# Reordered ends of the feed-forward stages and of the gated mixing, one-column bank marks, and named activation tables in a fused two-block layer kernel

## The reference

```python
def conv_ffn(h, w_up, conv_w, conv_b, w_down):            # ffn0
    u = h @ w_up
    up = jnp.pad(u, ((0, 0), (1, 1), (0, 0)))
    u = sum(up[:, j:j + t] * conv_w[j] for j in range(3)) + conv_b
    a, g = jnp.split(u, 2, axis=-1)
    return (jax.nn.gelu(a) * g) @ w_down                   # hidden width 2816
def swiglu_ffn(h, w_in, w_out):                            # ffn1 to ffn4
    gate, up = jnp.split(h @ w_in, 2, axis=-1)
    return (jax.nn.silu(gate) * up) @ w_out
def gmlp_chunk_mix(h, w_uv, v_norm, w_s, b_s, w_o):        # gated mixing
    z = jax.nn.gelu(h @ w_uv)
    u, v = jnp.split(z, 2, axis=-1)                        # 2048 columns each
    v = rms_norm(v, v_norm)
    ws = jnp.where(causal[None], w_s, jnp.zeros_like(w_s))                   # 16 groups of 128 x 128
    sv = jnp.einsum('gts,bcsgd->bctgd', ws, v) + jnp.transpose(b_s)[:, :, None]
    return (u * sv) @ w_o
```

## Time and profile before

| | |
|---|---|
| median of three timed runs | 1980.64 us (1976.95 to 1982.74) |
| the profiled execution | 1974.38 us, of which the span is 1972.2 us |
| mean granted TensorE clock | 0.992 of full speed |
| busy TensorE | 1886.9 us (96% of the span) |
| busy VectorE | 1407.4 us (71%) |
| busy ScalarE | 1044.1 us (53%) |

### The profile page before, as it was taken

One profiled execution on the slowest core, in us unless ns is written; L12 is line 12 of the kernel. 1 busy time (PEld: TensorE's weight loads), 2 busy tenths in 40 slices (PEclk: granted clock), 3 DMA queues, 4 the chain that ended last, 5 costly groups with the idle time before them and its releaser, 6 DMA issues. The chain is left out here.

```text
span 1972.2 us, 40546 instructions
## 1 busy us (share of the span) xinstructions
PE 1886.9 (96%) x16839; PEld 1786.0 (91%) x16844; DVE 1407.4 (71%) x1786; ACT 1044.1 (53%) x1390; POOL 45.7 (2%) x42
## 2 busy tenths in 40 slices
PE   7999998999999999989987999999999998999998
PEld 7998997999998899989886999998999998999997
DVE  6685589767777877798565667778777756557776
ACT  6565576755556444568533554445444555545443
POOL 0000000000000000000052000000000000000000
PEclk9999999999999999999999999999999999999999
DMA  6843333354553455444401434554455453534552
GB/s 219 251 175 127 129 129 113 128 187 172 190 192 139 160 195 188 171 146 149 154 4 46 150 127 173 191 189 174 172 190 192 168 190 117 182 113 174 189 192 107
DMA packets 52316, 313.39 MB, mean 159 GB/s; under 512 B 13536, under 2 KB 13792, under 8 KB 14944
## 3 DMA queue, kind: packets, MB, share of 16 engines
q1 hardware_dynamic: 51760, 308.42, 44.2%
q10 hardware_dynamic: 432, 3.15, 0.4%
HBM read 310.50 MB, written 1.05 MB: 158 GB/s over the span
## 5 line engine op out<-in xcount | busy, mean ns | idle before, releaser
L2138 DVE TENSOR_TENSOR wl<-raw,wh 128x1024 fp32r<-128x1024 f32 x576 | 687.5, 1223 | 375.7 <-ACT wh L1462 372.8
L1462 ACT ACTIVATE wh<-raw 128x1024 fp32r<-128x1024 f32 x575 | 587.8, 1051 | 304.2 <-PE ps L308 154.8
L308 PE MATMUL ps<-pages_r,wh 128*128 128x256 f32 x2480 | 548.1, 287 | 34.1 <-DVE wl L2138 17.7
L308 PE MATMUL ps<-pages_r,wl 128*128 128x256 f32 x1680 | 479.0, 285 | 0.0
L308 PEld LDWEIGHTS ps<-pages_r,wh 128*128 128x128 f32 x2480 | 424.8, 195 | 38.8 <-issue 19.1
L308 PE MATMUL ps<-norm_r,wh 128*128 128x256 f32 x2336 | 430.2, 285 | 2.5 <-DVE norm_r L2202 1.7
L308 PEld LDWEIGHTS ps<-norm_r,wh 128*128 128x128 f32 x2336 | 365.9, 192 | 5.6 <-issue 2.0
L372 PE MATMUL ps<-norm_r,wh 128*128 128x512 f32 x1408 | 355.1, 394 | 2.6 <-DVE wl L2138 1.7
L308 PE MATMUL ps<-norm_r,wl 128*128 128x256 f32 x1184 | 335.0, 283 | 0.0
L308 PEld LDWEIGHTS ps<-pages_r,wl 128*128 128x128 f32 x1680 | 326.1, 194 | 0.0
L372 PEld LDWEIGHTS ps<-norm_r,wh 128*128 128x128 f32 x1408 | 253.5, 189 | 50.4 <-DVE wl L2138 2.4
(11 more groups left out here) (345 smaller groups left out, 1823.8 us busy)
## 6 DMA issues: line engine op xcount, KB each, us to landing
raw<-in_stream SPq DMA_DIRECT2D x287, 1024.0 KB, 4.8
pages<-in_rpb SPq DMA_DIRECT2D x32, 64.0 KB, 6.3
pages<-in_mem SPq DMA_DIRECT2D x2, 512.0 KB, 6.4
raw<-in_stream SPq DMA_DIRECT2D x2, 512.0 KB, 8.4
x<-in_x SPq DMA_DIRECT2D x1, 1024.0 KB, 12.3
pages<-in_mem ACTq DMA_DIRECT2D x1, 1024.0 KB, 5.0
pages<-in_gmlp_b ACTq DMA_DIRECT2D x1, 1024.0 KB, 4.5
pages<-in_gmlp_w ACTq DMA_DIRECT2D x1, 1024.0 KB, 6.6
```

What stands on the lines that cost most here:

```text
L308: mm = pe.matmul(out, left, right, start=start and q == 0, stop=stop and q == 2, skip_group_check=True)
L1462: f(t.wh[(2 * b0 + hf) % PIECE_SLOTS][:], t.raw[b0 % 2][:, hf * 1024:(hf + 1) * 1024], ACT.Copy).then_inc(s["high_done"], 1)
L2138: tt(t.wl[i][:], t.raw[b0 % 2][:, hf * 1024:(hf + 1) * 1024], t.wh[i][:].bitcast(F32), ALU.subtract).then_inc(s["low_done"], 1)
```

## The change

It has four parts. What is computed stays the same, and so do the weight blocks, which come in another order.

1. **Ends of the feed-forward stages.** In the last step of each stage, `early` (the scaling of the gate) goes ahead of the first weight split; the second split is done in halves, and the hidden product goes between them (`between`), ahead of the second half. In ffn0 the step with the taps goes ahead of the first half and the product between the halves. ScalarE's order follows: in ffn0 the gelu and the high copy come right behind the second block's high copies.
2. **Bank marks.** The four matmuls at L469 write one column of each bank.
3. **Gated mixing.** The order of the stream is two gate blocks, eight value blocks, then the other six gate blocks as a new segment `gm_w`. The mixing quarters stand between its blocks, as `MIX_BEHIND` says: two quarters behind the second block, then one, two, two and one behind the following. The mask product stands behind the first two gate evacuations, ahead of the splits of the value blocks. VectorE and ScalarE follow that order: evacuation of a gate block, splits of a later one, then the quarters that are due; VectorE waits for the gelu of gate block q at quarter q, where it waited for all eight before.
4. **Named sets.** `preload_act_table_set("natural_log_exp_and_others")` is put at the start of ScalarE's program, ahead of the Ln of each norm root, of the four logarithms in the `w_in` stage, of the root of the scan's norm, of RWKV's decay exponentials, and in place of the dummy Ln for `rw_o`. It loads one table set that holds both Ln and Exp.

```diff
     ("rw_r", 4, 5), ("lora2", 0, 1), ("mem2_v", 4, 4), ("rw_v", 4, 4), ("rw_o", 4, 4), ("xq0", 4, 4), ("xo0", 4, 4),
-    ("ffn2", 44, 33), ("ffn3", 44, 33), ("gm_u", 8, 8), ("gm_v", 8, 8), ("gm_o", 4, 8),
+    ("ffn2", 44, 33), ("ffn3", 44, 33), ("gm_u", 2, 2), ("gm_v", 8, 8), ("gm_w", 6, 6), ("gm_o", 4, 8),
     ("xq1", 4, 4), ("xo1", 4, 4), ("ffn4", 44, 33),
...
 WOVEN = 18
+MIX_BEHIND = (0, 1), (2,), (3, 4), (5, 6), (7,)
 SEG, BLK = {}, {}
...
         for bank in range(4, 8):
-            pe.matmul(ps[:, bank, :], t.zrow[:, :], t.zrow[:, 0:1].broadcast_to([P, 512]), start=True, stop=True,
+            pe.matmul(ps[:, bank, 0:1], t.zrow[:, :], t.zrow[:, 0:1], start=True, stop=True,
                       skip_group_check=True)
...
     norm_sum("mix2")
-    project("gm_u", norm_parts, first=2, n=2)
-    project("gm_u", norm_parts, first=4)
     project("gm_v", norm_parts, groups=2, token=True)
-    pe.wait_ge(s["gm_mask"], 1)
-    for q in range(8):
+    def mix_quarters(qs):
+        for q in qs:
+            mix_pair(q)
+    def mix_pair(q):
         if q % 2 == 0:
...
         mm.then_inc(s["gm_mix"], 1)
+    project("gm_w", norm_parts, n=2)
+    pe.wait_ge(s["gm_mask"], 1)
+    mix_quarters(MIX_BEHIND[0])
+    for k in range(2, 6):
+        project("gm_w", norm_parts, first=k, n=1)
+        mix_quarters(MIX_BEHIND[k - 1])
     for q in range(4):
...
     f = act.activation
+    act.preload_act_table_set("natural_log_exp_and_others")
...
+        act.preload_act_table_set("natural_log_exp_and_others")
         act.wait_ge(s["norm_sum"], NORM[name] + 1)
...
         eps = t.stat[:, COL_EPS:COL_EPS + 1]
+        act.preload_act_table_set("natural_log_exp_and_others")
         act.wait_ge(s["norm_sum"], NORM[name] + 1)
...
     def log(dst, src):
+        act.preload_act_table_set("natural_log_exp_and_others")
         f(dst, src, ACT.Ln).then_inc(s["hg_log"], 1)
...
     for q in range(4):
+        if q == 0:
+            act.preload_act_table_set("natural_log_exp_and_others")
         act.wait_ge(s["hg_var"], q + 1)
...
         b = BLK[seg]
+        trips = (FIT - 1) // 2
         late_norm(seg, prev)
...
                 step = (i * 2 + (1 + k), i * 4 + (2 + 2 * k), (1 + k) % 2, first and k == 0)
+                if k == 1 and isinstance(i, int) and i == trips - 1:
+                    early(*step)
+                    high(blk[0])
+                    if fi == 0:
+                        late(*step)
+                        high(blk[1])
+                        end(*step)
+                    else:
+                        high(blk[1])
+                        late(*step)
+                    high(blk[2])
+                    continue
                 high(blk[0])
...
-        trips = (FIT - 1) // 2
         if fi <= 1:
...
     act.wait_ge(s["rw_cum"], 1)
+    act.preload_act_table_set("natural_log_exp_and_others")
     f(t.page[3], t.page[3], ACT.Exp, scale=-RATE).then_inc(s["rw_exp"], 1)
...
         f(used_pairs(t, po, b, 1), made_pairs(t, po, 1), ACT.Copy).then_inc(s["rw_u_sb1"], 1)
-    f(t.stat[:, 42:43], t.stat[:, COL_EPS:COL_EPS + 1], ACT.Ln)
+    act.preload_act_table_set("natural_log_exp_and_others")
     for q in range(4):
...
     highs("gm_u", n=2)
+    act.preload_act_table_set("natural_log_exp_and_others")
     act.wait_ge(s["norm_sum"], NORM["mix2"] + 1)
...
     f(t.stat[:, 44:46], t.stat[:, 44:46], ACT.Exp, scale=-0.5).then_inc(s["gm_root"], 1)
-    for k in range(1, 9):
-        if 1 < k < 8:
-            high(BLK["gm_u"] + k)
-        c = slice((k - 1) * 512, k * 512)
-        act.wait_ge(s["u_evac"], SEG["gm_u"] + k)
+    def gate_gelu(k):
+        c = slice(k * 512, (k + 1) * 512)
+        act.wait_ge(s["u_evac"], (SEG["gm_u"] + k if k < 2 else SEG["gm_w"] + k - 2) + 1)
         f(t.pages[:, c], t.pages[:, c], ACT.Gelu_apprx_tanh).then_inc(s["gm_up"], 1)
+    gate_gelu(0)
+    gate_gelu(1)
     act.wait_ge(s["gm_root"], 2)
...
         f(t.page[3][:, c], t.page[3][:, c], ACT.Copy, scale=t.stat[:, 35:36]).then_inc(s["gm_vout1"], 1)
-    for page in range(2):
-        operand_high(f"gm{page}", t.page[7 + page], t.page_r[10 + page],
-                     lambda q: act.wait_ge(s["gm_mixed"], 4 * page + q + 1))
+    def gated_high(q):
+        page, c = q // 4, slice(q % 4 * 512, (q % 4 + 1) * 512)
+        act.wait_ge(s["gm_mixed"], q + 1)
+        f(t.page_r[10 + page][:, c], t.page[7 + page][:, c], ACT.Copy).then_inc(s["op_high"], 1)
+    high(BLK["gm_w"])
+    gate_gelu(2)
+    for k, behind in enumerate(MIX_BEHIND):
+        high(BLK["gm_w"] + 1 + k)
+        gate_gelu(3 + k)
+        for q in behind:
+            gated_high(q)
     highs("gm_o", n=7)
...
-    def hidden(fi, st, k, make):
+    def hidden(fi, st, k, make, between=lambda: None):
...
         make(t.work[:, k * 512:(k + 1) * 512])
+        between()
         dve.wait_ge(s["hidden_high"], st + (fi * FIT + 1))
...
                 blk = [i * 6 + (r + j) if isinstance(i, int) else At(i * 6 + (r + j), r + j) for j in range(3)]
+                if k == 1 and isinstance(i, int) and i == trips - 1:
+                    early(i * 2 + 2, 0)
+                    low(blk[0])
+                    if fi == 0:
+                        step(i * 2 + 2, i * 4 + 4, 0)
+                        low(blk[1], (0,))
+                        end(i * 2 + 2, 0, lambda: low(blk[1], (1,)))
+                    else:
+                        low(blk[1], (0,))
+                        step(i * 2 + 2, i * 4 + 4, 0, lambda: low(blk[1], (1,)))
+                    low(blk[2])
+                    continue
                 low(blk[0])
...
                 step(i * 2 + (1 + k), i * 4 + (2 + 2 * k), (1 + k) % 2)
-                if fi == 0 and k == 1 and isinstance(i, int) and i == trips - 1:
-                    end(i * 2 + (1 + k), (1 + k) % 2)
-                    low(blk[2])
-                    continue
                 low(blk[2])
...
-    def conv_hidden(st, k):
+    def conv_hidden(st, k, between=lambda: None):
         dve.wait_ge(s["gelu_ready"], st + 1)
         hidden(0, st, k, lambda out: tt(out, t.page[k][:, 0:512], t.page[k][:, 512:1024],
-                                        ALU.mult).then_inc(s["hidden_made"], 1))
+                                        ALU.mult).then_inc(s["hidden_made"], 1), between)
...
-        def step(st, tile, k):
+        def step(st, tile, k, between=lambda: None):
             gate = t.work[:, 1024 + k * 512:1536 + k * 512]
...
             dve.wait_ge(s["u_evac"], st * 4 + (n0 + 4))
-            hidden(fi, st, k, lambda out: tt(out, made, gate, ALU.mult).then_inc(s["hidden_made"], 1))
+            hidden(fi, st, k, lambda out: tt(out, made, gate, ALU.mult).then_inc(s["hidden_made"], 1), between)
...
-        dve.wait_ge(s["piece_done"], 2 * (BLK["gm_u"] + k) + 2)
+        n, b = (SEG["gm_u"] + k, BLK["gm_u"] + k) if k < 2 else (SEG["gm_w"] + k - 2, BLK["gm_w"] + k - 2)
+        dve.wait_ge(s["piece_done"], 2 * b + 2)
         scaled(t.pages[:, k * 512:(k + 1) * 512],
-               ps[:, (SEG["gm_u"] + k) % BANKS, :].rearrange("p (n t) -> p n t", n=2), 2).then_inc(s["u_evac"], 1)
+               ps[:, n % BANKS, :].rearrange("p (n t) -> p n t", n=2), 2).then_inc(s["u_evac"], 1)
...
     gate_half(1)
-    lows("gm_u", 2, 1)
     dve.wait_ge(s["rows_in"], 32)
...
        ALU.mult).then_inc(s["gm_mask"], 1)
-    for k in range(2, 8):
-        gate_half(k)
-        if k < 7:
-            lows("gm_u", k + 1, 1)
     low_groups("gm_v", 0, 2)
-    dve.wait_ge(s["gm_up"], 8)
     dve.wait_ge(s["gm_vnorm"], 8)
...
-    for q in range(8):
+    def mixed_quarter(q):
         dve.wait_ge(s["gm_mix"], q + 1)
...
         link(ins)
+        dve.wait_ge(s["gm_up"], q + 1)
         tt(t.pages[:, 7 * FP + q * 512:7 * FP + (q + 1) * 512], tmp, t.pages[:, q * 512:(q + 1) * 512],
...
             mixed_low(q - 1)
+    gate_half(2)
+    lows("gm_w", 0, 1)
+    for k, behind in enumerate(MIX_BEHIND):
+        gate_half(3 + k)
+        lows("gm_w", 1 + k, 1)
+        for q in behind:
+            mixed_quarter(q)
     mixed_low(7)
...
         "xq1": k_blocks(i["xattn_wq_2"][1]), "xo1": k_blocks(i["xattn_wo_2"][1]),
-        "gm_u": k_blocks(uv[:, :GM_W]), "gm_v": k_blocks(uv[:, GM_W:]),
+        "gm_u": k_blocks(uv[:, :512]), "gm_w": k_blocks(uv[:, 512:GM_W]), "gm_v": k_blocks(uv[:, GM_W:]),
         "gm_o": [x for pair in zip(*gm_o) for x in pair],
```

## The result

| | before | after |
|---|---|---|
| median of four executions each, taken together | 1978.80 us | 1953.94 us (1952.64 to 1955.66) |
| the profiled execution | 1974.38 us | 1955.66 us |
| its span | 1972.2 us | 1953.9 us |

The ratio is 0.9873, with a 95% interval from 0.9853 to 0.9894: 24.9 us less between the medians, where 23.1 were forecast, and a median of 1953.9 where 1957.5 was. (The forecast started from a median of 1980.64 us over three executions; with the fourth it is 1978.80, and half of the distance to 1957.5 is that.) The same kernel in another session had a median of 1951.85 us, a ratio of 0.9875 (0.9860 to 0.9890). The two profiled executions lie only 18.7 us apart: the one of before is among its fastest, the one of after is the slowest of its four. Much of what follows is about that difference.

What follows compares the result with a forecast made beforehand. TensorE, busy 1886.9 of 1972.2 us, was taken as the bound. Feed-forward ends 5.6, marks 2.2, gated mixing 8.0 and named sets 7.3 make 23.1 us: median 1980.64 to 1957.5, range 1951 to 1963 (1949 to 1967 with rivals).

Steps and rivals of the forecast that it cites:

- C: Gated mixing: value blocks first and quarters spread between gate blocks win 8.0 us, bounds 0 to 8.5.
- A: Ends of the feed-forward stages: earlier low part of the last hidden tile wins 5.6 us, from 3.5 to 6.5.
- 0.80 was missing: Ends of ffn1 to ffn4: low part comes at least 1.2 us sooner, closing each 0.80 us hole; 3.2 us.
- ScalarE now has its conv middle ahead of the high copy: End of ffn0: ScalarE's conv middle of 1.10 us precedes the high copy, which then ends near 597.8.
- B: Bank marks: one column instead of 512 wins 0.55 us in each of four stages, 2.2 us (0 to 3.5).
- Rival 1: Bank marks: they cost by the instruction, not the column, so their gain falls away: 1959.7 us; chance 0.08.
- Rival 2: Gated mixing: VectorE paces the stretch and its whole gain is lost: 1965.5 us; chance 0.11.
- D: Named sets: no table load between Ln and Exp on chains that are waited for; 7.3 us, from 4 to 9.
- if a repeat is carried out and not dropped, three loads, mostly beside TensorE's work: w_in stage: repeated preloads cost ScalarE at most 3.8 us, mostly beside TensorE's work.
- rival 4: w_in stage: preloads repeated in full delay weight splits, 3.8 us back: 1961.3 us; chance 0.08.
- Rival 3: Table loads: a set change hides another 1.28 us, so removed loads give 5.1 us more: 1952.4 us; chance 0.03.
- rivals 5 and 6: 5: VectorE, next bound, takes gains back, 1976 us, chance 0.05; 6: mixing becomes one serial chain, 2012.7 us, chance 0.03.

Runs made afterwards that it cites:

- `after_again`: The changed kernel run again with no edit: 1951.85 us, ratio 0.9875 against the kernel before.
- `mix_last`: The changed kernel with all eight mixing quarters behind the last gate block: 1957.56 us, ratio 0.9900.
- the control: The changed kernel run again unaltered, in one session with three of the follow-up kernels: 1951.85 us, ratio 0.9875.
- `tail_loads`: The changed kernel with two more table loads between Ln and Exp of the last norm root: 1955.00 us, ratio 0.9881.

## Why the prediction was right

**The sum.** 24.9 us between medians against 23.1. The mechanisms held, but part of the agreement is luck: errors that cancel. C won more than forecast, and more than its upper bound of 8.5; the clock behind ffn0's hole gave back less, in some executions; and 1.6 us were lost in `w_in`, where the forecast had nothing. That loss is one of the prediction's own signs of being wrong ("if ScalarE runs late in w_in"): it came, and was too small to show in the sum.

**A, feed-forward ends: 5.6 forecast.** The mechanism held at all five places. In ffn1 to ffn4 the step "0.80 was missing" undersized the gain. At each of the four places TensorE gains 0.95 us at the last down product itself and 1.06 by the second product behind it. (The lines of ffn2 to ffn4 in the table hold other gains too.) With 0.94 for ffn1, as its line has it, and 1.06 for the others that is 4.1 in all where 3.2 stood. Matmuls start 0.12 us apart but last 0.28, and the first behind a hole lasts 0.39, so a hole costs some 0.25 us more than its bracket says. Of the two moves, it is the half split that does the work (0.69 of 0.80), not the earlier scaling. In ffn0 the hole was forecast at 1.9 us and is 1.90. That the clock would hold behind it was wrong for the profiled execution: the windows view gives, for the 4 us behind the hole, first in that profile and then in `after_again`,

```profile
609.87:613.87 4.00, 4.00 (x23) 4.00 (x24) 2.81 (x3) 1.68 (x3) 0.00 (x0) 0.66 0.79 289
```

```profile
607.68:611.68 4.00, 4.00 (x33) 4.00 (x34) 3.57 (x5) 1.77 (x4) 0.00 (x0) 1.00 0.82 283
```

the same kernel and the same hole, 23 matmuls against 33. Of the seven profiles with this hole it fell in four. From the matmul at 600 us in the first profile to the start of ffn1 (617.67 there) the kernel before took 18.6 us, the changed one 16.2 where the clock held and 17.7 where it fell: 2.4 us were won in some executions and 0.9 in others. The hole's length, nearer to 1.66 than to 3.02, did not decide it. The step "ScalarE now has its conv middle ahead of the high copy" was costed rightly and then taken as given; it was the whole of the hole.

**B, marks: 2.2 forecast.** The price was nearer the other bound: 0.69 us per stage, not 0.55. But one of the four stages counted, ffn0, gives it back by its last down product, so ffn2 to ffn4 make 2.1. The sum came out right with the wrong stages. The cover that was not asked about: with VectorE late at the end of the stage, anything won ahead on TensorE is waited for there. Rival 1 is out.

**C, gated mixing: 8.0 forecast, 9.06 measured.** The term that was mis-sized is the pace of the mixing matmuls, 0.126 us from a row at the end of a stall, where they run at 0.111: 7.1 us for 64, and 16.1 - 7.1 = 9.0. All that was named as cover held; no gate block waits for its splits. Rival 2 is out for the quarters as they are spread, and `mix_last` shows the price it feared: 4.3 us.

**D, named sets: 7.3 forecast.** Place by place, from the two profiles: start 0.7 (0.5), ffn1 with the marks 1.1 (1.4), mix1 1.4 (1.3), key norm 1.4 (1.3), rw_o 1.4 (1.3), tail 1.1 to 1.3 (1.3). That is 7.2 us. (For the key norm the control is used, whose clock fell twice behind mix1's norm as before; the table's 2.84 holds some 1.5 us for a fall less. The hole of 0.61 at the start of ffn1 did not close but shrank to 0.22.) What was wrong is the step "if a repeat is carried out and not dropped, three loads, mostly beside TensorE's work". They are carried out, they stand ahead of two high copies, and TensorE lost 1.6 us by them; with one load in place of four it was 1.8 us ahead at the same place. So rival 4 came true as a mechanism beside the forecast, at under half its price of 3.8 us. What the forecast did not follow is who waits there: VectorE's splits wait for ScalarE's high copies, and these stood behind the loads. Rival 3 fell by `tail_loads`, rivals 5 and 6 by the result.

**What the profiles alone would have said.** The parts make 4.1 + 1.6 (ffn0, marks and end) + 1.8 (marks of ffn2 to ffn4, as read there) + 9.1 + 7.2 - 1.6 = 22.2 us; the two spans differ by 18.3. In between lie 5.1 us in the scan and 0.8 at the branch outputs against it, and some 2.2 us for it where the clock was low for longer before than after (behind mix1's norm, at rw_o); that leaves 18.5. None of these is shown to belong to the change. The medians, where such things are averaged over executions, differ by 24.9, which is 2.7 us more than the parts: within what they can tell.

## What to carry to other kernels

When the last operand of a stage is late, look at what its engine does between the product and the last conversion: work that fits into the wait for the partner engine is free, work ahead of it is paid in full. Then ask the same of the partner's queue, since the 2.17 us left in ffn0 were an order on ScalarE that cost nothing to change. A saving on the bounding engine counts only up to the next place where it waits for another, and a table preload belongs only where the set is really changed.

## What the runs showed of the hardware

- A table load costs 1.28 us on ScalarE and no more, also with another right behind it (1944.48, 1945.77, Exp at 1947.06), and a preload is carried out in full when its set is already in place (113.83, 122.12 and 125.35 in the changed kernel).
- A matmul of one column with bf16 operands takes 0.05 us of TensorE's time (0.19 for four), one of 512 columns 0.22.
- The same hole in the same program may or may not be followed by the lower clock. Behind the hole of 1.9 us in ffn0 it fell in 4 of 7 profiles, behind one of 2.1 us near the 310th microsecond in 8 of 14, behind one of 2.1 us near the 151st in 4 of 9. Behind the hole of 1.66 us that answers to 1692.35 it fell in none, behind that of 2.39 us at 859.74 and behind or within all longer ones in every profile. Length alone does not decide: among the small matmuls of the scan it fell behind pauses of 1.44 us in two profiles (0.72 in the 6 us from 993 with wide marks, 0.66 in the 5 us from 1001 with the new mixing order alone). A fall cost 1.5 us in ffn0, 0.8 at the 151st microsecond, and between nothing and 1.5 near the 310th, and so is part of the scatter between executions.
- One pause of TensorE put down to "issue" in the RWKV scan comes in steps of 0.27 us and differs between executions of one program (0.90 and 0.63 us at the same instruction); the cause of these pauses was not tried.
